# Expert stage of a two-layer trunk: from one expert per 128-row tile to steps of two 64-row lanes

## What is computed

```python
g_p, g_i = lax.top_k(softmax(t @ rg_w + rg_b), 1)          # one group of 4
e_p, e_i = lax.top_k(softmax(e_logits[rows, g_i]), 2)      # two of its 4 experts
w = g_p * e_p / sum(e_p)
hid = silu(t @ w_gate[e]) * (t @ w_up[e])                  # 1024 -> 256
y   = sum over the two experts of w * (hid @ w_down[e])    # 256 -> 1024
```

## Time and profile before

| | |
|---|---|
| median of 3 runs | 2176.97 us (2176.8 to 2179.28) |
| the profiled execution | 2177.04 us, span 2175.2 us |
| PE busy | 2034.2 us (94%), granted clock 0.969 on average |
| DVE, ACT, POOL busy | 948.7, 492.6, 128.0 us |
| HBM | 303.52 MB read, 58.52 MB written |

### The profile page before, as it was taken

The page is one execution under the profiler, slowest core; times in us unless marked ns, Lnnn a source line. Parts: engine busy times, 40 slices in busy tenths (PEclk is TensorE's granted clock), DMA queues, the critical chain, the costliest instruction groups (busy, mean ns, idle before and its releaser), DMA issues.

```text
span 2175.2 us, 23007 instructions
## 1 busy us (share of the span) xinstructions
PE 2034.2 (94%) x9027; PEld 1376.8 (63%) x9027; DVE 948.7 (44%) x1998; ACT 492.6 (23%) x791; POOL 128.0 (6%) x193
## 2 busy tenths in 40 slices
PE   5999999999999997999589999999999999799993
PEld 2787776667777783444258777666776668544441
DVE  1135028667756863111252531476676128511115
ACT  1241113434410011111134310134344000111112
POOL 2000000000000002000210000000000000200001
PEclk9999999999999998999889999999999999799997
DMA  9661112333264337999661111142323430699974
GB/s 358 227 228 47 31 47 80 124 102 103 69 213 145 136 116 296 360 354 362 251 189 58 60 36 39 32 134 88 117 83 113 145 106 40 227 346 364 353 295 164
DMA packets 172698, 360.93 MB, mean 166 GB/s; under 512 B 11536, under 2 KB 124816, under 8 KB 161648
## 3 DMA queue, kind: packets, MB, share of 16 engines
q1 hardware_dynamic: 145808, 269.43, 35.8%
q0 software_dynamic: 19408, 64.70, 8.2%
q10 hardware_dynamic: 7376, 25.33, 2.9%
HBM read 303.52 MB, written 58.52 MB: 166 GB/s over the span
## 4 chain that ended last, share of the span: by engine, by line
PE 80%; DMA 10%; DVE 5%; issue 1%; ACT 1%; POOL 1%; SPq 1%; ACTq 0%; DVEq 0%; POOLq 0%
PE PS L979 75%; DMA ring<-in_expert_w_up_dram 6%; PE PS L983 4%; DMA ar<-in_ada_w_dram 1%; DVE ar L1576 1%; POOL rows L955 1%; DMA mg<-rows 1%; DMA xr<-out_y_dram 1%; DMA br<-rows,posi 1%; DVE xr L535 1%; PE PS L682 1%; DMA rows<-br,posi 1%; ACT hT L1374 0%; SPq L813 0%; DVE br L1576 0%
## 5 line engine op out<-in xcount | busy, mean ns | idle before, releaser
L979 PE MATMUL PS<-hT,ring 128*128 128x320 f32 (+1 forms) x2624 | 719.5, 439 | 5.8 <-DVE hT L672 4.2
L979 PEld LDWEIGHTS PS<-hT,ring 128*128 128x128 f32 (+1 forms) x2624 | 486.6, 189 | 214.9 <-issue 11.2
L979 PE MATMUL PS<-ring,mg 128*128 128x512 f32 (+1 forms) x1552 | 554.2, 512 | 25.0 <-DMA ring<-in_expert_w_up_dram 11.6
L979 PEld LDWEIGHTS PS<-ring,mg 128*128 128x128 f32 x1552 | 291.3, 192 | 234.7 <-issue 205.1
L535 DVE SCALAR_TENSOR_TENSOR xr<-ring,cs,xr 128x256 f32<-128x256 f32 x560 | 246.7, 482 | 9.9
L979 PE MATMUL PS<-br,ring 128*128 128x320 f32 x768 | 215.6, 434 | 0.8 <-DVE br L1773 0.8
L979 PEld LDWEIGHTS PS<-br,ring 128*128 128x128 f32 x768 | 145.1, 190 | 64.2 <-issue 4.2
L1576 DVE TENSOR_TENSOR mg<-PS,mg 128x256 f32<-128x256 f32 x38 | 16.1, 424 | 380.5 <-ACT mg L1374 380.5
L1374 ACT ACTIVATE xr<-PS 128x256 f32<-128x256 f32 (+1 forms) x108 | 56.0, 524 | 553.7 <-PE PS L979 553.6
L979 PE MATMUL PS<-ring,hT 128*128 128x256 f32 x800 | 177.4, 381 | 1.7 <-DVE ar L1576 1.7
L979 PEld LDWEIGHTS PS<-ring,hT 128*128 128x128 f32 x800 | 150.5, 190 | 26.2 <-issue 5.6
(11 more groups left out here) (229 smaller groups left out, 1465.6 us busy)
## 6 DMA issues: line engine op xcount, KB each, us to landing
ring<-in_w_in_dram SPq DMA_DIRECT2D x50, 1024.0 KB, 7.9
ring<-in_ada_w_dram SPq DMA_DIRECT2D x40, 1024.0 KB, 5.2
ring<-in_expert_w_gate_dram SPq DMA_DIRECT2D x38, 1024.0 KB, 8.5
ring<-in_expert_w_up_dram SPq DMA_DIRECT2D x38, 1024.0 KB, 10.6
ring<-in_expert_w_down_dram SPq DMA_DIRECT2D x38, 1024.0 KB, 5.3
rows<-br ACTq DMA_DIRECT2D x38, 512.0 KB, 8.9
mg<-rows SPq DMA_DIRECT2D x36, 512.0 KB, 11.4
rows<-const POOLq DMA_DIRECT2D x1, 13824.0 KB, 55.1
```

Source lines behind the costliest of these rows:

```text
L979: return nc.tensor.matmul(out, lhsT, rhs, start=start, stop=stop, skip_group_check=True)
```

## The change

A step keeps its 128 rows but has two lanes of 64. Step s has the first 64 rows of expert s in lane 1; lane 0 takes a further half tile of expert s, s-1 or s-2, which is the guest. For that the weights of four experts stay resident (`HOMES` = 4): `ring`, `hT` and `br` become one tensor `store`, in which expert e has home e % 4. What does not fit goes to extra tiles of 128 rows from 16 on, of which the first is now written out as step 16. Step 0 is expert 0 alone. Matmuls of steps 1 to 15 come in pairs, one for each lane, with 64 stationary columns and the guest's weights at an address from a register, read from `exi` ahead of each step. Three tiles come by token list instead of two: the lists of tiles 1 and 2 are made from `posi`, with their matmuls inside `gate_up(0)`, and POOL gathers them between the scatters. Residual and weights of the combination move behind step 0 on VectorE. `rows` has 35 tiles instead of 27. `ys` moves into `ar`.

```diff
-TILES = 26
+TILES = 34
-DIRECT = 2
+DIRECT = 3
+HOMES, HOME = 4, 3 * BLK
+LANE = P // 2
...
-                for e in range(DIRECT, NE):
+                for e in range(2, NE):
                     on.wait_filled(sp, ("gu", e - 2))
                     for part in range(2):
-                        strip_load(e, e % 2, part)
+                        strip_load(e, e % 2, part, e % HOMES)
+                    if e == 2:
+                        sp.wait_ge(on.scattered, 16 * 2 * T)
                     on.wait_filled(sp, ("xg", e - 1))
                     rows_load(e + 1, (e + 1) % 2)
                     on.wait_filled(sp, ("dn", e - 2))
-                    down_load(e, e % 2)
+                    down_load(e, e % 2, e % HOMES)
...
+                pool.wait_ge(on.route_ready, FIRST_LISTED)
+                listed_rows(0)
                 pool.wait_ge(on.route_ready, PLACES)
                 for t in range(T):
+                    if 1 <= t < DIRECT:
+                        pool.wait_ge(on.route_ready, PLACES + t)
+                        if t == 2:
+                            on.wait_filled(pool, ("xg", 0))
+                        listed_rows(t)
                     for w in range(2):
...
+                def lanes_gate_up(s):
+                    on.wait_moved(pe, ("xg", s))
+                    on.wait_block(pe, ("gate", s))
+                    on.wait_block(pe, ("up", s))
+                    own = strips(slice(HOME * (s % HOMES), HOME * (s % HOMES) + 2 * BLK))
+                    guest = strips(bass.ds(guests[s], 2 * BLK)) if s else None
...
+                    for k in range(KD):
+                        if s == 0 and k in (3, 5):
+                            listed(k // 2)
+                        if s == 0:
+                            last = mm(out, xgT[0][:, k, :], own[:, k, :, :], k == 0, k == KD - 1)
+                        else:
+                            mm(out[0:LANE], xgT[s % 2][:, k, 0:LANE], guest[:, k, :, :], k == 0, k == KD - 1)
+                            last = mm(out[LANE:P], xgT[s % 2][:, k, LANE:P], own[:, k, :, :], k == 0, k == KD - 1)
...
-                for j in range(NE):
+                for j in range(NE + 1):
+                    if j == 1:
+                        pe.wait_ge(on.route_ready, LANES)
+                    if 1 <= j < NE:
+                        guests[j] = pe.value_load(exi[0:1, j:j + 1], min_val=0, max_val=HOME * (HOMES - 1))
                     on.wait_slot(pe, ("gu", j))
-                    gate_up(j, 0)
+                    if j < NE:
+                        lanes_gate_up(j)
+                    else:
+                        gate_up(j, 0)
...
-                with pe.Fori(NE // 2, TILES // 2) as i:
+                with pe.Fori(NE // 2, TILES // 2 - 1) as i:
...
-                gate_up(2, pairs - 1)
-                rows_turned(3, pairs - 1)
-                down(1, pairs - 1)
-                hidden_turned(2, pairs - 1)
                 down(2, pairs - 1)
...
                 rows_moved(0, 0)
+                for s in range(1, DIRECT):
+                    here = R["here"][:, 2 * T * (s - 1):2 * T * s]
+                    step(V.tensor_scalar(here, R["pos"], 1.0 - LANE - P * s, None, ALU.add))
+                    tt(seat[s].rearrange("p (n s) -> p n s", n=2 * T), bc(cst("slot").unsqueeze(1), [P, 2 * T, P]),
+                       bc(here.unsqueeze(2), [P, 2 * T, P]), ALU.is_equal).then_inc(on.masks_ready, 1)
+                for s in range(1, DIRECT):
+                    listed(s)
+                lanes_listed()
```

More of the change, by code:

```diff
@@ L215, in build_tables @@
     job("D", "rank")
[L216 to L217 removed]
+    job("D", "idx", 0)
     job("D", "xg", 0)
+    for s in range(1, DIRECT):
+        job("D", "idx", s)
     moe_block = len(blocks)
@@ L379, in build_program @@
                             ("eq", 80), ("run", 80), ("m1", 5), ("m2", 5), ("dq", 5), ("M", 160),
-                            ("rk", 96), ("rr", DIRECT * T), ("cmp", 64), ("nt", 16), ("end", 16), ("shift", 16),
-                            ("at", 80), ("pos", 10), ("ex", TILES + 1), ("exc", (TILES - NE) * NE), ("pairs", 4)):
+                            ("rk", 96), ("rr", T), ("cmp", 9 * NE), ("halves", 16), ("over", 16), ("lane", 16),
+                            ("first", 16), ("held", 16), ("left", 16), ("end", 16), ("back", 16), ("jump", 16), ("at", 80), ("pos", 10),
+                            ("here", 10 * (DIRECT - 1)), ("token", DIRECT), ("from", 16), ("home", 16), ("ex", TILES + 1), ("exc", (TILES - NE) * NE), ("pairs", 8)):
             R[name] = ar[:, at:at + width]
@@ new lines, in _ @@
+                listed(0)
+                on.wait_moved(dve, ("rank",))
+                halves, over, lane, first, held, left, end, back, jump = (
+                    R[n] for n in ("halves", "over", "lane", "first", "held", "left", "end", "back", "jump"))
+                cmp9, cmp5 = (R["cmp"][:, 0:n * NE].rearrange("p (e j) -> p e j", e=NE) for n in (9, 5))
+                ramp = slot[:, 0:NE]
+                step(V.tensor_scalar(halves, R["rk"][:, NE * T:NE * (T + 1)], 1.0 / LANE, None, ALU.mult))
@@ new lines, in _ @@
+                step(tt(cmp9, bc(halves.unsqueeze(2), [P, NE, 9]), bc(slot[:, 0:9].unsqueeze(1), [P, NE, 9]), ALU.is_gt))
+                step(V.tensor_reduce(over, cmp9, AXL.X, ALU.add))
+                step(V.tensor_tensor_scan(lane, ramp, over, 0.0, ALU.max, ALU.add))
+                step(tt(first, lane, over, ALU.subtract))
+                step(V.scalar_tensor_tensor(out=held, in0=slot[:, HOMES - 1:HOMES - 1 + NE], scalar=NE + 1.0, in1=first, op0=ALU.min, op1=ALU.subtract))
+                step(V.scalar_tensor_tensor(out=held, in0=held, scalar=0.0, in1=over, op0=ALU.max, op1=ALU.min))
@@ new lines, in _ @@
+                step(tt(left, halves, held, ALU.subtract))
+                step(tt(cmp5, bc(left.unsqueeze(2), [P, NE, 5]), bc(slot[:, 0:9:2].unsqueeze(1), [P, NE, 5]), ALU.is_gt))
+                step(V.tensor_reduce(left, cmp5, AXL.X, ALU.add))
+                step(V.tensor_tensor_scan(end, cst("ones")[:, 0:NE], left, float(NE), ALU.mult, ALU.add))
+                step(tt(back, end, left, ALU.subtract))
+                step(V.scalar_tensor_tensor(out=back, in0=held, scalar=-0.5, in1=back, op0=ALU.mult, op1=ALU.add))
@@ new lines, in _, with per_token, by_token @@
+                step(tt(jump, first, ramp, ALU.subtract))
+                step(V.tensor_scalar(jump, jump, float(P), -float(P), ALU.mult, ALU.add))
+                def per_token(row):
+                    return bc(row.unsqueeze(1), [P, T, NE])
+                def by_token(name):
+                    return R[name][:, 0:T * NE].rearrange("p (t e) -> p t e", t=T)
+                rk3, at3, el3, eq3, run3 = (by_token(n) for n in ("rk", "at", "el", "eq", "run"))
+                step(V.scalar_tensor_tensor(out=at3, in0=rk3, scalar=float(LANE), in1=per_token(jump), op0=ALU.is_ge, op1=ALU.mult))
```

253 lines of the change are left out of this document (144 added, 109 removed).

## The result

The changed kernel takes **2155.53 us** (median of 4 runs, 2154.36 to 2157.69), beside 2176.89 for the kernel before on the same chip: a ratio of 0.9904, 95% interval 0.9892 to 0.9916. Its profiled execution has a span of 2152.5 us, 22.7 less than the span of before. Faster was right; of the 36.4 us forecast, about 15 did not come.

What follows compares the result with a forecast made beforehand. TensorE and DMA were taken as nearly balanced at 11.5 to 12 us a step, so the number of steps counts. Gains 44.1 and 1.7, losses 4.6 and 4.8, make 36.4 us: 2177.0 to 2141 us, range 2120 to 2164.

Steps and rivals of the forecast that it cites:

- rival 3: Start of the expert stage is DMA-bound, step 3 comes 8 us late in both layers: 2152 us, chance 0.08.
- Steps: Expert stage: 17 steps a layer instead of 19, at 12.07 us each, 44.1 us gained over both layers.
- the four changes: Switches between 64-column passes and 128-column transposes within a step: 0.15 us each, 0.6 us a step.
- no longer waited for: Expert weights: at 12.07 us a step, weights 11.5 us under way would no longer hold up TensorE.
- Pairs: Gate, up and down in steps 1 to 15: two 64-column passes cost one full pass, no extra time.
- rival 1: Paired narrow passes overlap only in part: 2295 us with half the overlap, 2450 with none; chance 0.04.
- Register read: Guest's place read on TensorE's queue each step: covered by down, costs nothing; 0.5 to 1.9 us a step uncovered.
- The start: Start of the expert stage: later places and scatter make step 3 2.3 us late a layer, 4.6 us lost.
- the sign that I had named: Step 3 beginning after 878 would show the forecast wrong; near 870 would show it right.
- 13.5 MB: Transfers queued from 835 on at the stage's start: at 386 GB/s, 35 us, so expert 3's strips at 870.
- The end: Eight empty rounds of the extra-tile loop ahead of the last down: 2.4 us lost a layer, 4.8 in all.
- the stall before its last step: Layer 1's last gate and up should have no stall ahead any more: 1.7 us gained.

Runs made afterwards that it cites:

- Start and end: Changed kernel with the empty extra-tile loop branched around, four scatters ahead of list 1's gather, expert 2's strips requested right after list 0's gather: 2140.28 us.
- Two lists: Changed kernel with two token lists instead of three, tile 2's rows again read from the scattered table: 2167.37 us.
- loop skipped: Changed kernel with one branch on each engine around the loop over further tiles when there are none: 2147.81 us.
- Two changes fewer: Changed kernel with the hidden tile's transposes moved behind gate and up of the next step, so all ten transposes stand together: 2158.31 us.
- full passes: Changed kernel with gate, up and down of steps 1 to 15 as 128-column passes, guest expert's computation left out: 2146.89 us.

## Why the prediction was right, and where it failed

The direction and the range were right, and the number of steps and their length, which make the gain, were reasoned as they came. The forecast itself was not met: 2141 against 2155.5. The time lies inside the range because the range was drawn past rival 3, not because the start was understood.

**Steps: right.** 17 groups in both layers. A step was forecast at 12.07 us and its mean is 12.07 and 12.08. It is 11.99 unhindered, and 0.15 us more than before stands in each of its four parts (7.02 for 6.87, 1.02 for 0.87, 3.58 for 3.44, 0.37 for 0.22), as the mixer's rows said. So the four changes cost 0.59, as the sum had it. But the 11.47 to which it added them held 0.07 of a restart behind a wait (the four parts make 11.40), and the mean holds 0.08 of waiting for up, in three steps of each layer: that these two cancel is luck, and "no longer waited for" was too much. (Up was 11.0 us under way in the earlier trace rows, from 1942.45 to 1953.48, not 11.5.) From step 3 to the last it is 156.8 and 158.6 us, 156.9 forecast; layer 1's 1.7 us more are step 3 itself, whose gate and up take 8.78 us at a granted clock of 0.80.

**Pairs: right.** 32 passes take 7.02 us, 16 pairs of 0.43, so rival 1 fell. The Trainium skill (TensorE: Matmul & The Clock Gate, Measured speedup vs the span model) has three column tiles of 32 columns at 2.38 times; no run here has three, and two of 64 gave twice.

**Register read: right.** In the changed kernel the read for the next step starts at 894.4, when down (894.21 to 897.79) has just begun:

```profile
L1410 PEldq TENSOR_LOAD <-exi x1: 296/296/296, 894.4 to 894.4; - x1
```

**The start: this step failed**, and here rival 3 came closer than the forecast: it had step 3 8 us late in both layers and 2152 in all. I forecast 2.3 us a layer; it was 6.4 and 9.2 (8.3 and 9.2 from step 0 on), that is 11.0 of the 13.7 us that the profile misses. The issue times were right or better (posi 825.5, last scatter 845.0; forecast 827 and 848), and step 3 stayed ahead of 878, the sign that I had named. What failed is the one division that stood for the stage, 13.5 MB from 835 on at 386 GB/s, so 870 for the strips of expert 3 and for step 3. First, the engines moved 356 GB/s from 835 to 874, at a share of 0.96: 13.9 MB in 39 us, and the strips landed at 873.9, not 870. Second, the scatter, the rows of tile 3 and then transposes and down follow one another: 856.6 + 10.0 + 7.5 = 874.1, where my sum gave the rows no time behind a landing at 855. In layer 0 the two end within 0.3 us of each other, so shortening one alone would have gained hardly anything there; in layer 1 the strips alone end it.

That nothing of the 13.5 MB was moved before 835 was in the sum. What I did not ask is what that costs: the engines were 0.42 and 0.29 busy from 826 and 1878 on, while POOL waited for a list. Start and end, which fills that stretch, takes 41.6 and 43.1 us from step 0 to step 3, so it got back 5.6 and 5.7 of the 8.3 and 9.2; where the rest is lost, no run separates. Two lists shows that a third list is still worth its wait.

**The end: the right size, with a part not foreseen.** Forecast 2.4 us a layer; layer 0 lost 2.7, of which the wait is 1.2 (3.21 for 2.02) and 1.6 the last down at half clock. Layer 1 lost 1.1 in the wait (3.16 for 2.10), had no such drop of the clock and, with the stall before its last step gone (1.7 us), came out 0.9 ahead.

**Between the layers: not in the sum.** 2.3 us were lost in layer 1's mixer, which the change does not touch; 2.0 of them are the group of the last section.

Term by term: steps 44.1 forecast, 42.4 measured; starts -4.6 and -15.6; ends with the stall -3.1 and -1.8; between the layers 0 and -2.3.

## What to carry to other kernels

When a step waits for something that is late, follow the whole chain of what must land one after another (scatter, rows, transposes, down) as well as the bytes; a sum of bytes at full rate is only a lower bound. An in-order queue that waits for a computed list can leave the DMA engines idle meanwhile (0.42 and 0.29 busy here), and in a stage that is 0.9 busy afterwards there was no place to make up for it: put what needs no list ahead of the wait. An empty loop directly ahead of the last matmuls can be paid twice, in the wait and, as in layer 0 here, in the clock behind it. And when the order of a step is changed, look at what the loads' queue waits for: with down at the end of the step the next weights were asked for later, and the mean step stayed where it was.

## What was not expected of the hardware

In layer 1's mixer a group of 128 matmuls (1775 us in the changed kernel) lasts 27.89 us in some profiles and 29.58 in others, for the same work. In the chains of the changed kernel and of loop skipped, each with the wait ahead of it from TensorE's timeline:

```profile
1775.25 29.58 PE PS L991 x128
...
1775.25 1.49 PE L991 MATMUL PS<-store,mg 128*128 128x256 f32 x5 [2.18 <-DVE mg L1640]
```

```profile
1771.36 27.89 PE PS L992 x128
...
1771.36 1.35 PE L992 MATMUL PS<-store,mg 128*128 128x256 f32 x5 [1.83 <-DVE mg L1643]
```

Ahead of it TensorE waits for VectorE, 1.83 us in seven of the fourteen kernels that were profiled and 2.18 or 2.19 in the others. Behind 1.83 it was always 27.89; behind 2.18 it was 29.58 in six of seven, with the granted clock at 0.50 from 1777 to 1779 in the changed kernel. So 0.35 us more of waiting went with 1.7 us lost at half clock in six profiles, and with nothing in one; what sets the two apart is not shown. Which kernels have the longer wait is not explained: no edit touches that place, and it stays open.

The change of pass width costs the same 0.13 to 0.15 us with 512 moving columns as with 128. Two changes fewer leave the mean at 12.0, where full passes reach 11.66 with the same bytes: in both about every other step waits for up, but the step without a wait is 11.7 us in the one and 11.4 to 11.5 in the other. What is left of the difference, some 0.1 us, was not settled.
